# Attention with its probabilities scaled on GpSimd and V held stationary on two halves of the array

## The reference, cut to what matters

```python
# 32 query heads and 4 key/value heads of 64; a group is one key/value head with its 8 query heads
q, k, v = split(rms_norm(x) @ w_qkv); q, k = rope(rms_norm(q)), rope(rms_norm(k))
kw, vw = (previous block of 128, own block) of k and v         # two blocks of 128 queries
scores = where(valid, q @ kw.T * 64 ** -0.5, -inf)
m      = maximum(max(scores, -1), sink)                        # sink: one number per head
p      = exp(scores - m)
probs  = p / (sum(p, -1) + exp(sink - m))
x      = x + (probs @ vw) @ w_o
```

## Time and profile before

| | |
|---|---|
| median of 3 runs | 2034.56 us |
| profiled execution, its own time | 2034.4 us |
| its span, first to last instruction | 2032.6 us |
| TensorE matmul / VectorE / ScalarE / GpSimd busy | 98% / 62% / 52% / 10% of the span |

### The profile page before, as it was taken

The page is one execution under the profiler, slowest core; times in us unless marked ns, Lnnn a source line. Parts: engine busy times, 40 slices in busy tenths (PEclk is TensorE's granted clock), DMA queues, the critical chain, the costliest instruction groups (busy, mean ns, idle before and its releaser), DMA issues.

```text
span 2032.6 us, 25932 instructions
## 1 busy us (share of the span) xinstructions
PE 1991.4 (98%) x9504; PEld 1659.7 (82%) x9504; DVE 1267.7 (62%) x1727; ACT 1065.8 (52%) x1356; POOL 201.3 (10%) x91
## 2 busy tenths in 40 slices
PE   7999999999999999999999998999999999999999
PEld 6888878888888888888887886888888888888887
DVE  5699956545968777785667674544454454444443
ACT  6444456546667585864547673544444444433332
POOL 0899740000000000000000000000000000000000
PEclk9999999999999999999999998999999999999999
DMA  8655545565545454545564333656655565656654
GB/s 296 194 186 184 171 132 195 168 207 166 156 154 154 143 160 134 156 134 176 166 207 137 113 109 110 197 189 195 191 189 189 173 197 191 193 192 191 194 193 159
DMA packets 182841, 352.69 MB, mean 174 GB/s; under 512 B 11616, under 2 KB 12000, under 8 KB 182752
## 3 DMA queue, kind: packets, MB, share of 16 engines
q1 hardware_dynamic: 181184, 350.27, 54.3%
q10 hardware_dynamic: 1568, 1.23, 0.2%
HBM read 349.36 MB, written 2.10 MB: 173 GB/s over the span
## 4 chain that ended last, share of the span: by engine, by line
PE 80%; DVE 11%; ACT 5%; issue 2%; DVEq 1%; DMA 0%; ACTq 0%; SPq 0%
PE acc L377 24%; PE acc L379 24%; PE acc L378 24%; DVE T L1030 7%; PE T L478 3%; PE T L359 2%; ACT w_hi L637 1%; DVE w_lo L975 1%; DVEq L967 1%; ACT sm L904 0%; PE T L488 0%; PE T L487 0%; PE T L558 0%; PE T L442 0%; ACT E L812 0%
## 5 line engine op out<-in xcount | busy, mean ns | idle before, releaser
L975 DVE TENSOR_TENSOR w_lo<-raw,w_hi 128x1024 fp32r<-128x1024 f32 x576 | 699.2, 1223 | 607.2 <-ACT w_hi L637 599.9
L637 ACT ACTIVATE w_hi<-raw 128x1024 fp32r<-128x1024 f32 x656 | 683.5, 1058 | 537.2 <-PE acc L379 518.7
L377 PE MATMUL acc<-w_hi,h_hi 128*128 128x512 f32 x1888 | 746.8, 396 | 15.0 <-DVE h_lo L987 13.0
L379 PE MATMUL acc<-w_hi,h_lo 128*128 128x512 f32 x1888 | 737.2, 390 | 0.0
L378 PE MATMUL acc<-w_lo,h_hi 128*128 128x512 f32 x1888 | 736.5, 390 | 0.0
L377 PEld LDWEIGHTS acc<-w_hi,h_hi 128*128 128x128 f32 x1888 | 355.7, 188 | 88.8 <-DVE h_lo L987 13.0
L379 PEld LDWEIGHTS acc<-w_hi,h_lo 128*128 128x128 f32 x1888 | 355.1, 188 | 74.8
L378 PEld LDWEIGHTS acc<-w_lo,h_hi 128*128 128x128 f32 x1888 | 355.8, 188 | 70.9
L346 POOL TENSOR_TENSOR w_lo<-raw,w_hi 128x1024 fp32r<-128x1024 f32 x80 | 189.8, 2408 | 89.9 <-ACT w_hi L637 89.6
L1030 DVE SCALAR_TENSOR_TENSOR T<-vpad,feat,T 128x256 f32<-128x256 f32 x464 | 182.4, 479 | 0.0
L377 PE MATMUL acc<-w_hi,y_hi 128*128 128x512 f32 x384 | 154.5, 402 | 7.4 <-DVE w_lo L975 5.2
(11 more groups left out here) (200 smaller groups left out, 1364.9 us busy)
## 6 DMA issues: line engine op xcount, KB each, us to landing
raw<-in_hgrn_w_in_dram SPq DMA_DIRECT2D x160, 512.0 KB, 3.6
raw<-in_conv_w_in_dram SPq DMA_DIRECT2D x96, 512.0 KB, 3.9
raw<-in_ffn_w_gate_dram SPq DMA_DIRECT2D x88, 512.0 KB, 4.4
raw<-in_ffn_w_up_dram SPq DMA_DIRECT2D x88, 512.0 KB, 4.2
raw<-in_ffn_w_down_dram SPq DMA_DIRECT2D x88, 512.0 KB, 4.7
raw<-in_attn_w_qkv_dram SPq DMA_DIRECT2D x40, 512.0 KB, 3.9
raw<-in_conv_w_out_dram SPq DMA_DIRECT2D x32, 512.0 KB, 4.2
raw<-in_hgrn_w_out_dram SPq DMA_DIRECT2D x32, 512.0 KB, 4.9
```

Source lines behind the costliest of these rows:

```text
L377: nc.tensor.matmul(o, hi[:, kt, a], w_hi[:, slot, kk, :], start=kt == 0, stop=False)
L379: last = nc.tensor.matmul(o, lo[:, kt, a], w_hi[:, slot, kk, :], start=False, stop=kt == p.chunks * CK - 1)
L637: A(w_hi[:, slot, :, :], raw[:, slot, :, :], ACT.Copy).then_inc(hi_ready, 1)
L975: TT(w_lo[:, slot, :, :], raw[:, slot, :, :], rounded(w_hi[:, slot, :, :]), ALU.subtract).then_inc(split_ready, 1)
```

## The change

- `mix_v`: V (128 keys x 64 channels) is the stationary operand and the turned P moves. Head 2i writes partitions 0 to 63 of the output and head 2i+1 partitions 64 to 127, so the output already has channels on partitions. Four matmuls for two heads (256 and 128 moving columns each) replace six of 64 columns.
- `y_turn` and `finish` are gone. The division is applied to P instead: VectorE takes the reciprocal (`inverse(g, i)`, tick e+10+i) and GpSimd multiplies P with it in place (four `tensor_scalar` for two heads) before `turn_p(g, i)`, which stays at tick e+8+i and now waits for `a_n`.
- The sink is a column beside each block of scores, so that the maximum and the sum of the exponentials include it. `maxima` loses two small operations, ScalarE loses L907, and each `exps(g, i)` ends with a drain. `masked(g, 0)` gains two small copies.
- `scores` issues two heads in turn. `PT` has four buffers in place of two.
- `y_out_hi` and `y_low` work on half a group each, at ticks e+13 and e+15; `att_out` waits for halves, and its order ends with chunks (0,6), (1,6), (0,7), (1,7). `x_turn(1)` comes at tick 59 in place of 60, `x_turn(0)` at 57 in place of 56, `x_hi(1)` at 62 in place of 60.

The diff, cut: runs of four and more removed lines, which stand in the functions printed above, are left out.

```diff
-        head = [(k, c) for cs in (range(chunks - 4), (chunks - 4, chunks - 3), (chunks - 2, chunks - 1))
+        head = [(k, c) for cs in (range(chunks - 4), (chunks - 4, chunks - 3), (chunks - 2,), (chunks - 1,))
 ...
+def late(name, k):
+    return 2 if name == "att_out" and k == 1 else 0
 ...
-        sm = sb(yl2, "sm", [P, 8, 3 * P])
-        PT = sb(yl2, "PT", [P, 2, 3 * P])
+        sm = sb(yl2, "sm", [P, 9, 4 * P])
+        PT = sb(yl2, "PT", [P, 4, 3 * P])
 ...
+        def with_sink(h):
+            s = sm[:, :, :].rearrange("p a b -> p (a b)")
+            return s[:, 4 * P * h + P - 1:4 * P * h + 2 * P], s[:, 4 * P * h + 2 * P:4 * P * h + 4 * P + 1]
 ...
+            for g in range(4):
+                for i in range(4):
+                    pool.wait_ge(a_inv, 4 * g + i + 1)
+                    for h in (2 * i, 2 * i + 1):
+                        for tb, s in enumerate(probabilities(h)):
+                            last = nc.gpsimd.tensor_scalar(s, s, ast[:, 6, 8 * tb + h:8 * tb + h + 1], None, ALU.mult)
+                    last.then_inc(a_n, 1)
 ...
-                    at.put(ph[name].end(k) + (4 if ph[name].last[k] == ph[name].last.get(0, 0) + 2 else 2),
+                    at.put(ph[name].end(k) + 2 + late(name, k) // 2,
 ...
 ...
+                for h in range(4 * half, 4 * half + 4, 2):
+                    heads = [(a, slice(HD * (a % 2), HD * (a % 2) + HD)) for a in (h, h + 1)]
+                    for a, r in heads:
+                        nc.tensor.matmul(T[:, a % 4, 0:P], aqT[r, a // 2, 0:P], kT[r, g, 0:P], start=True, stop=True)
+                    for a, r in heads:
+                        nc.tensor.matmul(T[:, a % 4, P:3 * P], aqT[r, a // 2, P:S], kT[r, g, :], start=True,
+                                         stop=True).then_inc(a_s, 1)
 ...
             def turn_p(g, i):
+                pe.wait_ge(a_n, 4 * g + i + 1)
                 for h in (2 * i, 2 * i + 1):
-                    pe.wait_ge(a_p, 8 * g + h + 1)
                     if 8 * g + h >= 2:
                         pe.wait_ge(a_ptc, 8 * g + h - 1)
                     if h < 2:
                         pe.wait_ge(a_sm, 8 * g + 8)
                     for b in range(3):
-                        last = nc.tensor.transpose(T[:, h % 2, b * P:(b + 1) * P], sm[:, h, b * P:(b + 1) * P], ident[:, :])
+                        last = nc.tensor.transpose(T[:, h % 2, b * P:(b + 1) * P], sm[:, h, (b + 1) * P:(b + 2) * P], ident[:, :])
                     last.then_inc(a_pt, 1)
             def mix_v(g, i):
 ...
+                pe.wait_ge(a_ptc, 8 * g + 2 * i + 2)
+                v = lambda tb: kvtok[:, tb, S + g * HD:S + (g + 1) * HD]
+                for tb in range(TB):
+                    for h in (2 * i, 2 * i + 1):
+                        o = T[HD * (h % 2):HD * (h % 2) + HD, 2 + i // 2, (i % 2) * S + tb * P:(i % 2) * S + S]
+                        w = PT[:, h % 4, 2 * P:3 * P] if tb else PT[:, h % 4, 0:2 * P]
+                        last = nc.tensor.matmul(o, v(tb), w, start=tb == 0, stop=tb == 1)
+                last.then_inc(a_o, 1)
 ...
-                if g:
-                    at.put(e + 5, lambda g=g: y_turn(g - 1))
                 at.put(e + 6, lambda g=g: scores(g, 0)).put(e + 7, lambda g=g: scores(g, 1))
                 for i in range(4):
                     at.put(e + 8 + i, lambda g=g, i=i: turn_p(g, i))
-                    at.put(min(e + 9 + i, 51), lambda g=g, i=i: mix_v(g, i))
-            at.put(51, lambda: y_turn(3))
+                    at.put(e + 9 + i, lambda g=g, i=i: mix_v(g, i))
             stream("kv_q", 0, h_hi, h_lo, x_turns("hgrn_out", 2, None).later(32).with_(at), normed(2))
             early = at.later(40)
 ...
+            stream("att_out", 0, y_hi, hy_lo, early.with_(x_turns("att_out", 3, (a_lo, 8))), lambda c: pe.wait_ge(a_lo, c + 1))
 ...
+                    at.put(e + 3, lambda k=k: x_squares(s, k)).put(e + 4 + late(name, k), lambda k=k: x_hi(s, k))
 ...
             def exps(g, i):
                 act.wait_ge(a_m, 2 * g + i // 2 + 1)
                 for h in (2 * i, 2 * i + 1):
 ...
+                    for tb, s in enumerate(with_sink(h)):
+                        k = 8 * tb + h
+                        A(s, s, ACT.Exp, bias=ast[:, 2, k:k + 1], accum_out=ast[:, 4, k:k + 1])
+                nc.scalar.drain().then_inc(a_p, 1)
             def p_copy(g, i):
                 for h in (2 * i, 2 * i + 1):
                     act.wait_ge(a_pt, 8 * g + h + 1)
 ...
+                    if 4 * g + i >= 2:
+                        act.wait_ge(a_o, 4 * g + i - 1)
+                    A(PT[:, h % 4, :], T[:, h % 2, 0:3 * P], ACT.Copy).then_inc(a_ptc, 1)
+            def y_out_hi(g, b):
+                act.wait_ge(a_o, 4 * g + 2 * b + 2)
+                A(flat(y_hi[:, 4 * g + 2 * b:4 * g + 2 * b + 2, :]), T[:, 2 + b, :], ACT.Copy).then_inc(a_hi, 1)
             at = Hooks()
             for g in range(-1, 4):
                 e = 16 + 8 * g
                 at.put(e + 2, lambda g=g: q_out(g)).put(e + 3, lambda g=g: q_std(g))
                 at.put(e + 9 if g < 0 else e + 7, lambda g=g: qk_copy(g))
-                if g > 0:
-                    at.put(e + 8, lambda g=g: y_out_hi(g - 1))
                 if g >= 0:
                     for i in range(4):
                         at.put(e + 10 + i, lambda g=g, i=i: exps(g, i))
                     for i in range(4):
                         at.put(e + 11 + i, lambda g=g, i=i: p_copy(g, i))
-            at.put(54, lambda: y_out_hi(3))
+                    for b in range(2):
+                        at.put(e + 13 + 2 * b, lambda g=g, b=b: y_out_hi(g, b))
 ...
+                    at.put(e + 2, lambda k=k: residual(name, k)).put(e + 5 + late(name, k), lambda k=k: x_lo(s, k))
 ...
             def masked(g, half):
+                if half == 0:
+                    if g:
+                        dve.wait_ge(a_pt, 8 * g)
+                    V.tensor_copy(sm[:, 0:8, P - 1], sinks[:, 8 * g:8 * g + 8])
+                    V.tensor_copy(sm[:, 1:9, 0], sinks[:, 8 * g:8 * g + 8])
                 for h in range(4 * half, 4 * half + 4):
                     dve.wait_ge(a_s, 8 * g + h + 1)
-                    if g and h == 0:
-                        dve.wait_ge(a_pt, 8 * g)
-                    STT(out=sm[:, h, :], in0=T[:, h % 4, 0:3 * P], scalar=HD ** -0.5, in1=wmask[:, :],
+                    STT(out=sm[:, h, P:4 * P], in0=T[:, h % 4, 0:3 * P], scalar=HD ** -0.5, in1=wmask[:, :],
                         op0=ALU.mult, op1=ALU.add).then_inc(a_sm, 1)
             def maxima(g, half):
-                if g and half == 0:
-                    dve.wait_ge(a_sink, g)
                 settle()
                 h = slice(4 * half, 4 * half + 4)
-                m, sink = (ast[:, r, :].rearrange("p (a b) -> p a b", a=2)[:, :, h] for r in (2, 3))
-                V.tensor_reduce(m[:, 0, :], sm[:, h, 0:P], AX.X, ALU.max)
-                V.tensor_reduce(m[:, 1, :], sm[:, h, P:3 * P], AX.X, ALU.max)
+                m = ast[:, 2, :].rearrange("p (a b) -> p a b", a=2)[:, :, h]
+                s = sm[:, :, :].rearrange("p a b -> p (a b)")
+                first, second = (s[:, a + 4 * P * 4 * half:a + 4 * P * (4 * half + 4)].rearrange("p (a b) -> p a b", a=4)
+                                 for a in (P - 1, 2 * P))
+                V.tensor_reduce(m[:, 0, :], first[:, :, 0:P + 1], AX.X, ALU.max)
+                V.tensor_reduce(m[:, 1, :], second[:, :, 0:2 * P + 1], AX.X, ALU.max)
                 settle()
 ...
                 V.tensor_scalar(m, m, -1.0, None, ALU.mult)
                 settle().then_inc(a_m, 1)
 ...
+            def inverse(g, i):
+                dve.wait_ge(a_p, 4 * g + i + 1)
+                l, inv = (ast[:, r, :].rearrange("p (a b) -> p a b", a=2)[:, :, 2 * i:2 * i + 2] for r in (4, 6))
+                V.reciprocal(inv, l).then_inc(a_inv, 1)
+            def y_low(g, b):
+                dve.wait_ge(a_hi, 2 * g + b + 1)
+                kk = slice(4 * g + 2 * b, 4 * g + 2 * b + 2)
+                low(flat(hy_lo[:, kk, :]), T[:, 2 + b, :], flat(y_hi[:, kk, :]), a_lo)
             at = Hooks()
             for g in range(-1, 4):
                 e = 16 + 8 * g
                 at.put(e + 2, lambda g=g: sums(g)).put(e + 5 if g < 0 else e + 4, lambda g=g: rope(g))
-                if g > 0:
-                    at.put(e + 6, lambda g=g: finish(g - 1)).put(e + 8, lambda g=g: y_low(g - 1))
                 if g >= 0:
                     for half in range(2):
                         at.put(e + 8 + half, lambda g=g, half=half: masked(g, half))
                         at.put(e + 8 + half, lambda g=g, half=half: maxima(g, half))
-            at.put(54, lambda: finish(3)).put(54, lambda: y_low(3))
+                    for i in range(4):
+                        at.put(e + 10 + i, lambda g=g, i=i: inverse(g, i))
+                    for b in range(2):
+                        at.put(e + 13 + 2 * b, lambda g=g, b=b: y_low(g, b))
```

(21 more changed lines are left out.)

3 lines of the change are left out of this document (removed).

## The result

| | before | after |
|---|---|---|
| median of 4 runs, us | 2034.54 (2034.24 to 2035.13) | 2052.90 (2051.68 to 2053.76) |
| profiled execution, own time and span, us | 2034.4 and 2032.6 | 2053.76 and 2052.0 |

The ratio is 1.0092, 95% interval 1.008 to 1.0104: the changed kernel is 18.4 us slower. The forecast of 2035.8 lay 17.1 us under it and the range ended at 2044, so the prediction was wrong.

What follows compares the result with a forecast made beforehand. TensorE, busy for 98% of the span, was taken to bound the kernel; 4.4 + 8.7 - 6.4 - 2.6 - 2.9 = +1.2 us gave a median of 2035.8 us, range 2029 to 2044.

Steps and rivals of the forecast that it cites:

- I take 1.5 ... Ends 0.7 and 2.2: GpSimd's four multiplications of P for two heads, 768 columns: 1.5 us, between writing alone (0.7) and two inputs (1.8).
- first wait: TensorE stands 4.8 us at each `turn_p(g,0)`, in all four groups, for `inverse(g,0)` on VectorE and then GpSimd.
- the period: Time of one attention group between `turn_p(g,0)` starts: from 37.4 to 40.3 us, 2.9 more, three times.
- the second wait: TensorE waits 2.5 us at `turn_p(g,3)` in groups 0 to 2, as `inverse(g,3)` stands behind `rope(g+1)`.
- The first rival: GpSimd's instructions and VectorE's `w_lo` or `rope` hold each other up: +9.1 us, 2044.9; chance 0.22.
- the price: GpSimd's time for two heads' multiplications, 1.5 us, entering seven times: four first waits, three second; ends -5.6 and +4.9.
- column halves run in turn: Rival: `mix_v`'s two heads do not overlap on TensorE, 1.3 us each, about +3: 2038.8; chance 0.15.
- The waits at the end of the last group: TensorE's waits of 1.89 and 2.01 us after the last attention group go; with `mix_v` and `y_turn`, -6.4 us.
- GpSimd is quick: Rival: GpSimd's multiplications run near its writing rate, 0.8 us each, 7 x -0.7 = -4.9: 2030.9; chance 0.13.
- the wait isn't there: Rival: the order on VectorE was read wrongly, so all savings count, 27.6 us: 2007; chance 0.05.
- The clock: Old low-clock stretches go with their stalls (4.6 us), new ones cost 1.7 in the last group: net -2.9 us.
- a second stretch: A second stretch at the low clock level after each new TensorE stall: up to +4 us.

Runs made afterwards that it cites:

- experiment 6: Changed kernel with `turn_p`, `mix_v`, `q_turn` one tick later in groups 0 to 2, `inverse(g,0)` and `inverse(g,1)` earlier, `rope` at e+13: 2025.57 us.
- experiment 8: Changed kernel without GpSimd's multiplication, and `mix_v` issuing both matmuls of one head, then both of the other: 2025.95 us, one run.
- experiment 9: Changed kernel with scaling on VectorE, `turn_p`, `mix_v`, `q_turn` later in groups 0 to 2, `rope` later, the last group's first two `inverse` earlier: 2016.36 us.
- experiment 2: Changed kernel with GpSimd multiplying by constant 0.5, in groups 2 and 3 as one instruction of 768 columns for two heads: 2050.84 us, one run.

## Why the prediction was wrong

**The step that failed** is the term "I take 1.5 ... Ends 0.7 and 2.2" for GpSimd's four instructions. They take 3.0 us alone, 3.5 to 4.0 beside `w_lo` and 4.9 beside `rope`. The upper end of 2.2 was above my own reading of two inputs at 1.8 us, and still too low: I took one input to be quicker than two, as the figure for writing alone suggested. It isn't: 2.5 ns a column against 2408 / 1024 = 2.35 for the two-input subtraction, with 0.2 to 0.3 us for each start on top. The 768 columns at the rate of the nearest row are 1.8 us; with four starts as measured since it is 2.6 to 3.0.

Where it bit, in group 1, from the rows above:

| stretch | forecast, us | measured, us |
|---|---|---|
| start of `scores(1,0)` to `inverse(1,0)` | 11.7 | 1146.81 - 1135.12 = 11.69 |
| that `inverse` to `turn_p(1,0)` | 0.2 + 1.6 | 1150.65 - 1146.81 = 3.84 |
| first wait | 4.8 | 6.55 |
| `turn_p(1,0)` to end of `inverse(1,2)` | 7.3 | 1158.69 - 1150.65 = 8.04 |
| from there to the next `w_lo`, over `rope` | 5.6 | 1164.54 - 1158.69 = 5.85 |
| that `w_lo` | 1.15 | 1.14 |
| `inverse(1,3)` and GpSimd to `turn_p(1,3)` | 1.8 | 1169.51 - 1165.68 = 3.83 |
| the period | 40.3 | 45.6, mean of three |

The order on VectorE was read rightly, to 0.1 us. Both excesses of 2.0 us are GpSimd's. The 0.7 in the fourth line is what the low clock adds to the transposes (1.54 for 0.88): the prediction had hidden that stretch inside the second wait, but the copies and exponentials start from those very transposes.

The miss of the profiled execution (2053.8 against 2035.6) is 18.2 us, and by the starts of `turn_p` it lies so. `turn_p(0,0)` started 5.6 us later than before (1104.92 and 1099.35), for a forecast of 4.4: 1.2 (2.0 by the chain, but the attention began 0.85 us earlier in this execution, `scores(0,0)` at 1089.39 against 1090.24, before anything that the change touches). Three periods longer by 5.3 each: 15.9. From `turn_p(3,0)` (1241.75; 1211.55 before) to the end 10.8 us were gained for a forecast of 11.9: 1.1, about what the longer stretch at the lower clock costs there (below).

**The first rival** (GpSimd and VectorE hold each other up) is true as a mechanism, and smaller than the price. I sorted GpSimd's 64 instructions by whether a VectorE instruction with two SBUF inputs ran beside them: 38 without one took 0.60 to 0.61 and 0.92 to 0.93 us, 26 with one took 0.60 to 1.59 (median 1.12) and 0.92 to 1.65. Beside VectorE's reductions nothing was lost. VectorE lost less: 1.33 us for a product that takes 1.22, and `rope` was late by 0.25 us, not by the 1.5 that the rival gave it. Of the seven sets on the chain five lose 0.5 us and two 0.9 and 1.0 (the first of the last group, the last of group 0). With `rope` that is some 5 us, where the price itself is 7 x 1.5 = 10.5. The rule of the Trainium skill (SBUF — State Buffer, Who interferes with whom), that a VectorE instruction with two SBUF inputs and a GpSimd one that reads SBUF contend, agrees with these rows in who interferes. What it costs by them is at most 1.0 us for one of GpSimd's instructions in this kernel, and often nothing; in experiment 6 it was 1.9 us once, beside two `w_lo` in a row. The price and the rival together explain between 15 and 16 us of the 18.2. The low clock is the rest, 0.7 in each period and an estimated 1.3 in the last group; with it the terms make 19, and the 0.85 us by which the attention began earlier brings them to the 18.2. That part is argued from the rows and was not tried alone.

**The other steps.** `mix_v` 0.80 (forecast 0.85): *column halves run in turn* is false by these 0.80 us, and experiment 8 shows it for the other order of issue. `scores` 1.51 (1.41). `x_turn(1)` waits 1.5 (1.3), and that part alone gains 4.3 (4.3). The waits at the end of the last group went, as forecast. *GpSimd is quick* and *the wait isn't there* are false. The second wait was placed at `turn_p(g,3)`, 2.5 us; it came split, 2.06 at `turn_p(1,2)` and 1.28 at `turn_p(1,3)`, because set 2 beside `rope` is itself late. The clock: I expected one stretch at the lower level after each first wait, at a cost of 1.7 us, which is one of 3.4. There is one at each, but it lasts 6.8 us in groups 0 to 2 and 10.3 in the last (1237.4 to 1247.7, at 0.50), and it begins while TensorE still waits. With TensorE at work it is 2.8 to 5 us of that in groups 0 to 2 and 5.95 in the last, which costs some 3.0 and not 1.7. Two more of 3.4 us follow the second waits of 3.04 (group 0) and 2.47 (group 2); a second stretch stood in the prediction only as an end, "up to +4". The granted clock over the 178 us is 0.89; with no wait over 1.5 in this stage (experiment 9) it is 1.00.

**The range** was too narrow by its own logic. The price entered seven times, so an upper end of 3 us would have put the edge at 2046, and with the first rival's 5 us as measured at 2051, still under the 2052.9. The ends of an operation that no row shows should have come from "as slow as the slowest near row, each start paid", not from a guess between two rows.

## What to carry to other kernels

Work given to an idle engine is not free when another engine waits for it: its duration counts once for every chain that it sits in, here seven times, and GpSimd's one-input fp32 multiplication is no quicker for a column than its two-input subtraction. Before moving work, ask which instruction releases it and what stands ahead of that in its in-order queue: the reciprocal behind a `masked` and a `w_lo` cost 3.0 us in each group, with no GpSimd at all. The gain could be had with the same mathematics: with the scaling on VectorE, `turn_p`, `mix_v`, `q_turn` and `rope` one tick later where that can be, and the last group's first two `inverse` earlier (experiment 9), it is 36.5 us faster than the changed kernel and 18 faster than the one before.

## What I had not expected of the hardware

- GpSimd, fp32 `tensor_scalar` in SBUF on 128 partitions: 0.60, 0.92 us for 128, 256 columns with the scalar from SBUF, 0.53, 0.85, 2.13 for 128, 256, 768 with a constant. VectorE does the first two in 0.28 and 0.35.
- It is slowed, up to 2.6 times (0.60 to 1.59; once 2.54, in experiment 6), beside VectorE instructions with two SBUF inputs. VectorE's were slowed by a tenth to a fifth (1.22 to 1.33, 0.69 to 0.81), and once, beside the wide instruction of experiment 2, to 1.77.
- Matmuls on two halves of the columns overlap in either order of issue: 0.80 and 0.81 us for work that is an estimated 1.3 us in turn.
